# A one-hot gate product in a mixture-of-experts layer: two single-pass matmuls of a split gate, spread over 24 slots a tile

## What is computed

```
q = (xb @ w_q).reshape(blk, PEER_HEADS, 2, PEER_HALF)
s = jnp.einsum('thpd,phkd->thpk', q, sub_keys)
sv, si = lax.top_k(s, PEER_TOPK)
cand = sv[:, :, 0, :, None] + sv[:, :, 1, None, :]
cand_idx = si[:, :, 0, :, None] * N_KEYS + si[:, :, 1, None, :]
top_s, top_pos = lax.top_k(cand.reshape(...), PEER_TOPK)
idx = jnp.take_along_axis(cand_idx..., top_pos, axis=-1)
g = jax.nn.softmax(top_s, axis=-1)
act = gelu(einsum('thk d,td->thk', u_tab[idx], xb))
y = einsum('thk,thkd->td', g * act, v_tab[idx])
```

## Time and profile before

| | us |
|---|---|
| median of 3 runs | 4426.57 (4424.93 to 4427.05) |
| profiled execution | 4427.57 |
| its span | 4425.5 |
| PE busy | 4175.6 (94%) |
| PEld busy | 3762.6 (85%) |
| DVE busy | 2527.9 (57%) |
| ACT busy | 1179.3 (27%) |
| granted clock of PE, mean | 0.961 of 2.4 GHz |

### The profile page before, as it was taken

One profiled execution on the slowest core, in us unless ns is written; L12 is line 12 of the kernel. 1 busy time (PEld: TensorE's weight loads), 2 busy tenths in 40 slices (PEclk: granted clock), 3 DMA queues, 4 the chain that ended last, 5 costly groups with the idle time before them and its releaser, 6 DMA issues. The chain is left out here.

```text
span 4425.5 us, 74733 instructions
## 1 busy us (share of the span) xinstructions
PE 4175.6 (94%) x27369; PEld 3762.6 (85%) x27369; DVE 2527.9 (57%) x4678; ACT 1179.3 (27%) x1585; POOL 38.2 (1%) x43
## 2 busy tenths in 40 slices
PE   8778679999999999999998988999999999999998
PEld 8654479999999998888888567999999998888887
DVE  3742247777776435555544846787777525555553
ACT  2101132233333321121113443223333322111111
POOL 0000000000000010000000000000000001000000
PEclk9868789999999999999998989999999999999998
DMA  3026523335445565555532012334454466555551
GB/s 111 19 92 202 170 84 105 112 126 185 154 160 171 186 233 193 193 193 194 189 112 71 24 38 96 107 123 142 165 181 157 166 209 218 192 195 190 196 190 53
DMA packets 321925, 652.38 MB, mean 147 GB/s; under 512 B 26241, under 2 KB 157442, under 8 KB 321154
## 3 DMA queue, kind: packets, MB, share of 16 engines
q1 hardware_dynamic: 318978, 642.36, 43.1%
q0 software_dynamic: 2816, 8.40, 0.5%
HBM read 509.00 MB, written 141.53 MB: 147 GB/s over the span
## 5 line engine op out<-in xcount | busy, mean ns | idle before, releaser
L1781 DVE TENSOR_TENSOR experts_ul<-experts_u,experts_uh 128x1024 fp32r<-128x1024 f32 x512 | 627.1, 1225 | 1074.4 <-ACT experts_uh L1678 1068.0
L1578 PE MATMUL ps<-peer_x_then_r_xh,experts_ul 128*128 128x260 f32 x4096 | 1173.3, 286 | 0.0
L1579 PE MATMUL ps<-experts_over_x_xl,experts_uh 128*128 128x260 f32 x4096 | 1157.4, 283 | 0.0
L1580 PE MATMUL ps<-peer_x_then_r_xh,experts_uh 128*128 128x260 f32 x4096 | 1155.8, 282 | 0.0
L1678 ACT ACTIVATE experts_uh<-experts_u 128x1024 fp32r<-128x1024 f32 x512 | 540.8, 1057 | 1094.7 <-PE ps L1642 1085.2
L1641 PE MATMUL ps<-experts_over_a_al,experts_uh 128*128 128x512 f32 x2048 | 797.3, 389 | 0.0
L1642 PE MATMUL ps<-experts_over_a_ah,experts_uh 128*128 128x512 f32 x2048 | 797.3, 389 | 0.0
L1640 PE MATMUL ps<-experts_over_a_ah,experts_ul 128*128 128x512 f32 x2048 | 797.2, 389 | 0.0
L1579 PEld LDWEIGHTS ps<-experts_over_x_xl,experts_uh 128*128 128x128 f32 x4096 | 772.9, 189 | 0.0
L1578 PEld LDWEIGHTS ps<-peer_x_then_r_xh,experts_ul 128*128 128x128 f32 x4096 | 772.1, 189 | 0.0
L1580 PEld LDWEIGHTS ps<-peer_x_then_r_xh,experts_uh 128*128 128x128 f32 x4096 | 771.9, 188 | 0.0
(11 more groups left out here) (342 smaller groups left out, 4770.0 us busy)
## 6 DMA issues: line engine op xcount, KB each, us to landing
experts_u<-peer_u SPq DMA_DIRECT2D x256, 512.0 KB, 3.3
experts_u<-peer_v SPq DMA_DIRECT2D x256, 512.0 KB, 3.3
hidden<-experts_act SPq DMA_DIRECT2D x256, 260.0 KB, 2.2
gates<-experts_over_b_g SPq DMA_DIRECT2D x128, 512.0 KB, 3.0
experts_over_b_g<-gates SPq DMA_DIRECT2D x128, 512.0 KB, 5.0
experts_act<-hidden SPq DMA_DIRECT2D x256, 256.0 KB, 3.6
mla_ct<-cache SPq DMA_DIRECT2D x64, 320.0 KB, 3.8
pa_ct<-cache SPq DMA_DIRECT2D x64, 320.0 KB, 3.8
```

Source lines behind the costliest of these rows:

```text
L1578: pe.matmul(o, ul[:, b % 4, c], xh[:, c, t], start=(c == 0), stop=False)
L1579: pe.matmul(o, uh[:, b % 4, c], xl[:, c, t], start=False, stop=False)
L1580: mm = pe.matmul(o, uh[:, b % 4, c], xh[:, c, t], start=False, stop=(c == KC - 1))
L1781: v.tensor_tensor(ul[:, b % 4], u[:, b % 2], uh[:, b % 4].bitcast(F32), ALU.subtract).then_inc(split_done, 1)
```

## The change

`hidden` and its 128 slots stay. What changes is what stands beside them.

- **The gate product.** `cols[:, 2]` (the gate) is split once a tile into `gate_h` (fp32r) and the rest, by a copy and a subtraction on DVE. `one_hot` makes onej (now fp32r, two buffers), onei (now one buffer), and then **two** products, one_h = onei x gate_h and one_l = onei x rest, both fp32r. `gates` does two fp32r matmuls for each token (onej by one_h, onej by one_l), 16 a batch in place of 8 in fp32.
- **The slots.** Tiles have 24 slots in place of 20: batches in two of three (b % 3 of 1 and 2), none where b % 3 is 0. The first tile begins at slot 24 (before 32) and 8 slots are left at the end (before 16).
- **DVE's order.** For each b: `one_hot` for the batch of slot b + 1 where (b + 1) % 3 is not 0, then `low`, then the pieces of the selection, which stand two together in every third slot: `{2: (0, 1), 5: (2, 3), 8: (4, 5), 11: (6, 7), 14: (8, 9), 17: (10, 11), 20: (12,)}`. The samples' selection moves from slots 16 to 23 to a place beside the fourth tile.
- **The turn of the picks** comes at the first slot of a tile, just before `hidden`, and one slot ahead of the first batch.
- **The stores of the gates** are issued four at once, after every sixth slot.
- `rest`, `top` and `topi` move to another shared buffer.

```
-FIND, PLAIN, BATCHES = 16, 4, TT // BT
-PER_TILE = PLAIN + BATCHES
-ONES = FIND + 2 * BT
+FIND, BATCHES = 16, TT // BT
+PER_TILE = BATCHES * 3 // 2
+ONES = FIND + 8
...
                 with sp.Fori(0, NP) as t:
...
+                    first = ONES + PER_TILE * t
+                    for b in range(PER_TILE):
+                        plain(first + b, b)
+                        if b % 6 == 5:
+                            for c in range(4):
+                                store_gates(PT * t + b // 6, b // 6 % 2, c)
+                for n in range(TAIL, NK):
...
-                    if n == TAIL + PLAIN:
+                    if n == TAIL:
                         for b in range(2):
                             sp.wait_ge(g_stored[b], 16 * 4 * NQ // 2 + 64)
...
                 def gates(n, b):

-                    pe.wait_ge(one_ready, n + 1)
+                    pe.wait_ge(one_ready, n + 2)
                     for m in range(2):
                         pe.wait_ge(g_free, 2 * n + m + 1)
                         for e in range(4):
-                            mm = pe.matmul(k.ps[:, 4 + m, e * NK:(e + 1) * NK], onej[:, b % 2, 4 * m + e], onei[:, b % 2, 4 * m + e],
-                                           start=True, stop=True)
+                            o, at = k.ps[:, 4 + m, e * NK:(e + 1) * NK], 4 * m + e
+                            pe.matmul(o, onej[:, b % 2, at], one_h[:, b % 2, at], start=True, stop=False)
+                            mm = pe.matmul(o, onej[:, b % 2, at], one_l[:, b % 2, at], start=False, stop=True)
                         mm.then_inc(g_ready, 1)
...
                 with pe.Fori(0, NP) as t:
                     first = ONES + PER_TILE * t
...
+                    turn_picks(t)
+                    with pe.Fori(0, 2) as v:
+                        for b in range(PER_TILE // 2):
+                            if b % 3:
+                                a_ = b - 1 - b // 3
+                                gates(BATCHES * t + BATCHES // 2 * v + a_, a_)
+                            hidden(first + PER_TILE // 2 * v + b, b)
+                turn_picks(NP)
...
+                with act_e.Fori(0, NP) as t:
                     first = ONES + PER_TILE * t
+                    for b in range(PER_TILE):
+                        v = b // 6
+                        if b % 6 == 1:
+                            act_e.wait_ge(g_stored[v % 2], 64 * (2 * t + v // 2) + 64)
+                        if b % 3:
+                            a_ = b - 1 - b // 3
+                            copy_gates(BATCHES * t + a_, a_, v)
                         plain(first + b, b)
+                        if b == 10:
+                            exponentials(t + 1)
...
+                def one_hot(n, at, b):
+
+                    tok = slice(at, at + BT)
+                    v.wait_ge(g_ready, 2 * n + 2)
+                    v.tensor_tensor(onej[:, b % 2], bc(k.iota[:], 1, BT), bc(cols[:, 1, tok], 2, NK), ALU.is_equal)
+                    wait(v, one_ready, n + 1)
+                    v.tensor_tensor(onei[:], bc(k.iota[:], 1, BT), bc(cols[:, 0, tok], 2, NK), ALU.is_equal).then_inc(one_made, 1)
+                    wait(v, one_made, n + 1)
+                    v.tensor_tensor(one_h[:, b % 2], onei[:], bc(gate_h[:, tok].bitcast(F32), 2, NK), ALU.mult)
+                    v.tensor_tensor(one_l[:, b % 2], onei[:], bc(cols[:, 2, tok], 2, NK), ALU.mult).then_inc(one_ready, 1)
...
+                with v.Fori(0, NP) as t:
+                    chain = Chain(v, elink)
+                    first = ONES + PER_TILE * t
+                    v.wait_ge(turned, t + 1)
+                    v.tensor_copy(cols[:], turn).then_inc(cols_copied, 1)
+                    wait(v, cols_copied, t + 1)
+                    v.tensor_copy(gate_h[:], cols[:, 2]).then_inc(gate_ready, 1)
+                    wait(v, gate_ready, 2 * t + 1)
+                    v.tensor_tensor(cols[:, 2], cols[:, 2], gate_h[:].bitcast(F32), ALU.subtract).then_inc(gate_ready, 1)
+                    wait(v, gate_ready, 2 * t + 2)
+                    for b in range(PER_TILE):
+                        if (b + 1) % 3:
+                            a_ = b - b // 3
+                            one_hot(BATCHES * t + a_, BT * a_, a_)
+                        low(first + b + LOW, b + LOW)
+                        for piece in PIECES.get(b, ()):
+                            select(piece, t + 1, t + 1, chain, STEPS * (t + 1))
```

More of the change, by code:

```diff
@@ L1302, in peer_experts @@
         cols = s.sb("cols", [P, 3, TT])
+        gate_h = s.sb("gate_h", [P, TT], F32R)
         scols = s.sb("scols", [P, 3, TS])
@@ L1317, in peer_experts @@
         rows = over.row().sb("rows", [P, TS, D])
-        over = Overlay(nc, s, "over_a", 16384)
+        over = Overlay(nc, s, "over_a", 4 * 7 * BT * NK)
+        found = over.row()
+        rest = found.sb("rest", [TT, NT, NK])
+        top = found.sb("top", [TT, NT, TOPK])
+        topi = found.sb("topi", [TT, NT, TOPK], U32)
         first = over.row()
-        onej = first.sb("onej", [P, 2, BT, NK])
-        onei = first.sb("onei", [P, 2, BT, NK])
+        onej = first.sb("onej", [P, 2, BT, NK], F32R)
+        onei = first.sb("onei", [P, BT, NK])
+        one_h = first.sb("one_h", [P, 2, BT, NK], F32R)
+        one_l = first.sb("one_l", [P, 2, BT, NK], F32R)
         then = over.row()
@@ L1326, in peer_experts @@
         al = then.sb("al", [P, 2, TP], F32R)
-        over = Overlay(nc, s, "over_b", 33280)
+        over = Overlay(nc, s, "over_b", 32768)
         first = over.row()
@@ L1376, in peer_experts @@
         cols_copied = s.sem("cols_copied")
+        gate_ready = s.sem("gate_ready")
         one_made = s.sem("one_made")
@@ L1464, in plain @@
                     store(n, b)
[L1466 to L1470, removed]
-                with sp.Fori(0, NP) as t:
[L1472 to L1481, removed]
+                for n in range(FIND, ONES):
+                    plain(n, n)
+                with sp.Fori(0, NP) as t:
+                    first = ONES + PER_TILE * t
[5 more added lines that the diff above has]
+                for n in range(TAIL, NK):
                     if n + LOAD < NK:
@@ L1731, in exponentials @@
                     act_e.activation(expd[:], expd[:], ACT.Exp).then_inc(exped, 1)
[L1733 to L1739, removed]
                 def plain(n, b):
@@ L1743, in plain @@
                     gelu(n, b)
-                def tile(t, last=False):
-                    first = ONES + PER_TILE * t
-                    for b in range(PLAIN):
-                        plain(first + b, b)
[L1749 to L1760, removed]
+                for n in range(FIND, ONES):
+                    plain(n, n)
+                    if n == FIND + 4:
+                        exponentials(0)
+                with act_e.Fori(0, NP) as t:
+                    first = ONES + PER_TILE * t
+                    for b in range(PER_TILE):
[5 more added lines that the diff above has]
+                            copy_gates(BATCHES * t + a_, a_, v)
+                        plain(first + b, b)
+                        if b == 10:
+                            exponentials(t + 1)
                 for n in range(TAIL, NK):
@@ L1784, in _ @@
                 v.sem_inc(score_free, 1)
+                v.sem_inc(one_ready, 1)
                 slab_low(0, 0)
@@ L1908, in choose @@
                     assert chain.n == STEPS, chain.n
-                choose(0, NP, FIND, 0)
-                v.wait_ge(turned, 1)
+                choose(0, 0, FIND, 0)
+                def one_hot(n, at, b):
[7 more added lines that the diff above has]
+                    v.tensor_tensor(one_l[:, b % 2], onei[:], bc(cols[:, 2, tok], 2, NK), ALU.mult).then_inc(one_ready, 1)
+                PIECES = {2: (0, 1), 5: (2, 3), 8: (4, 5), 11: (6, 7), 14: (8, 9), 17: (10, 11), 20: (12,)}
+                with v.Fori(0, NP) as t:
[15 more added lines that the diff above has]
+                            select(piece, t + 1, t + 1, chain, STEPS * (t + 1))
+                    assert chain.n == STEPS
+                v.wait_ge(turned, NP + 1)
                 v.tensor_copy(scols[:], turn[:, :, 0:TS]).then_inc(cols_ready, 1)
@@ L1919, in _ @@
                 v.tensor_scalar(h_idx[:], at_of[:], float(TP), None, ALU.add).then_inc(idx_ready, 1)
[L1920 to L1955, removed]
                 def gate(m, b, par):
```

8 lines of the change are left out of this document (2 added, 6 removed).

## The result

| | before | after |
|---|---|---|
| median, us | 4425.75 (run beside it) | 4478.05 (4474.11 to 4480.86) |
| ratio | | 1.0115 [1.0102, 1.0128] |
| profiled execution / span, us | 4427.57 / 4425.5 | 4480.86 / 4479.0 |
| PE busy | 4175.6 (94%) | 4188.3 (94%) |
| DVE busy | 2527.9 | 2672.1 |

What follows compares the result with a forecast made beforehand. PE's own stream was taken as the bound. Product 0, waits 55.8 us and restarts 5.6, less 11.3 + 0.8, gave net +49 us: 4476 us, 1.1% slower; own range 4465 to 4492, with rivals 4422 to 4528.

Steps and rivals of the forecast that it cites:

- What bounds the kernel: In the tiles PE's own stream is the bound; PE waits only where one_hot comes late, 11.3 us before the change.
- Part 1: Gate product: 16 fp32r matmuls cost a batch 1.76 to 1.80 us, as now, bound by weight loads; 0 us taken.
- Part 2: Steady part of a tile: low, two pieces, then a longer one_hot make PE wait, 5.87 us a tile.
- Part 3: A tile's start: PE waits 1.10 us for the first one_hot behind the turn, bounds 0.7 to 1.6.
- Part 4: Samples' selection, ACT's work and four stores at once cost nothing while their cover lasts.
- rival D: The burst of stores delays u, 1 to 2 us in 32 places: 4508 to 4540; chance 8%.
- The sum: Whole kernel: waits 55.8 us and restarts 5.6, less 11.3 + 0.8 that go; net +49 us, 4476 median.
- Restarts: After each PE wait in the tiles, 0.1 us more; 7 x 8 x 0.1 = 5.6 us.
- rival C: The clock falls at the larger waits beside half-streaming gates: 32 falls, +51 us, 4527; chance 6%.
- Rival A: Waits inside the tiles don't appear, low coming earlier or pieces being covered; only the start remains: 4424; chance 11%.
- B: Gate product: fp32r matmuls stream, not bound by the load; a batch falls to 0.94 us: 4366; chance 9%.
- The case on which 66% stood: The forecast itself: DVE's order and longer one_hot make PE wait, product unchanged; 4476 us, own range 4465 to 4492.

Runs made afterwards that it cites:

- the kernel with the pieces ahead: The kernel after, with the selection pieces moved before low on DVE in every third slot; 4422.38 us, ratio 0.999.
- the split product in the old slots: The kernel before, with the split, four operations and 16 fp32r matmuls, keeping its 20 slots, DVE order and spread stores; 4468.06 us, ratio 1.0092.

## Why the prediction was right, and where it was off

**What bounds the kernel**, and what an idle PE costs: held. No other engine than DVE, and no DMA, ended a wait of PE in the tiles.

**Part 1, 0 us for the product**: held, 0.11 us a load in fp32r too, with all 128 columns and with 32. The two rules of the Trainium skill's "TensorE: Matmul & The Clock Gate" part here. Its section "LDWEIGHTS (loading the stationary operand)" gives P / 1.2 ns for a load of P columns, from which 107 ns for 128 columns is an estimate, and the trace agrees (110 to 112). The 81 ns of "Back-to-back issue gap" are not reached by any batch of fp32 or fp32r here, not even with few columns: no two loads of a batch start less than 107 ns apart.

**Part 2, DVE's order**: this step carried the forecast and held. The waits by slot, from the start of `hidden` to the start of the next batch, less the 5.75 us without a wait, mean of 8 tiles:

| slot of the tile | forecast | measured |
|---|---|---|
| 1 (start) | 1.10 | 0.98 |
| 4 | 1.67 | 1.44 |
| 7 | 0.41 | 0.17 |
| 10 | 0.73 | 0.57 |
| 13 | 0.2 | 0.86 |
| 16 | 1.43 | 1.19 |
| 19 | 1.43 | 1.27 |
| sum | 6.97 | 6.48 |

Five of the six in the steady part are 0.16 to 0.24 too high. The part that they share is `low`, which begins 3.52 behind the batch (905.81 - 902.29) where 3.66 was taken; besides, some pairs are up to 0.08 shorter than they were taken (the first 5.11, 912.06 - 906.95, for 5.18). The one_hot's 4.97 came out as 4.96. Slot 13 is the term that was mis-sized: the forecast took ACT's way to `low` for the same in every triple, and ACT has the exponential in one of them, with a table load of 1.28 us ahead of it (968.03) and another behind. The first is on the path: the copies of the batch come behind it (969.54), `high` behind them (970.50), and `low` 0.86 us later than elsewhere. The second comes when `high` is done, and delays nothing: the gelu behind it waits another 2.10 us for PE. The Trainium skill's "ScalarE activation tables: per-element evaluation and per-set limits", section "What a function is on this engine", gives 1283 ns for such a load, and the trace agrees. The statement that ACT "has 207 of 577 us" and so costs nothing was an average over slots; in this one slot ACT was on the path.

**Part 3, the start**: 0.98 for 1.10. From the turn (887.68) to the one_hot 2.00 for 2.20.

**Part 4**: held, but for ACT's exponential. The gates' stores land in 4.4 us where they took 3.0, and neither PE nor ACT waits for a DMA in the tiles: rival D's burst is in the kernel with the pieces ahead too, at 4422.

**The sum.** Waits 6.48 x 8 = 51.8 for 55.8. Restarts: from the batch's start to `hidden` 1.83 us behind a wait and 1.74 without, 56 x 0.09 = 5.0 for 5.6. Less the 12.1 of the waits of before. That is 44.7. From the start of `hidden(16)` to that of `hidden(127)` the two layers take 1576.0 us where they took 1520.8, 55.2 more. The rest is **rival C, in part**: seven falls of the clock. One of them, behind the wait of 1.02 at slot 16 (windows; columns as in the earlier trace rows, PEclk the third from the right):

```profile
1003.00:1005.00 2.00, 1.52 (x14) 1.52 (x14) 2.00 (x3) 0.47 (x2) 0.00 (x0) 1.00 0.00 0
1005.00:1007.00 2.00, 2.00 (x14) 2.00 (x14) 1.90 (x3) 1.71 (x3) 0.00 (x0) 0.68 0.65 123
1007.00:1009.00 2.00, 2.00 (x12) 2.00 (x11) 2.00 (x2) 0.06 (x1) 0.00 (x0) 0.50 0.71 268
1009.00:1011.00 2.00, 2.00 (x18) 2.00 (x18) 1.36 (x2) 0.00 (x0) 0.00 (x0) 0.97 0.01 4
```

The clock goes to the lower level (1.2 GHz) for some 3 us, and `hidden` takes 7.33 us from 1005.32 to 1012.65 where it takes 5.8. All seven stand behind the waits at slots 4, 16 and 19. They cost 7 x 1.53 = 10.7, and 44.7 + 10.7 = 55.4 for 55.2. The spans differ by 53.5, since the rest of the program, in which the change only moves buffers, took 1.7 us less in this execution. The forecast gave C only as a whole case, 32 falls or none; a few falls belonged in the sum. It priced a fall at 1.6 us as 16 gate matmuls at half speed. The size is right, but by luck: the gate matmuls are over by 1005.32, and it is the `hidden` behind them that runs slowly. The waits and restarts were put 5 us too high and the clock 11 too low, so the total of +49 for +52 came out closer than its terms; that closeness is luck, the 56 waits are not.

Rival A (the waits don't appear) was refuted by the 56 waits, B by loads that stand 0.11 us apart with 128 columns and with 32, D by the burst that cost nothing. The case on which 66% stood is shown, not only argued: taking away the order alone ends the waits at slots 4 to 19, and taking away the fourth operation leaves 0.2 to 0.5 us of them at slots 4, 16 and 19.

## What to carry to other kernels

Where one engine feeds the one that bounds the kernel, an average of free time says little: write down when each operand is ready and when it is wanted, slot by slot, and put work whose inputs are there ahead of an operation that a third engine releases late. Here one moved call was worth 56 us. The gate products here, of 128 columns and fewer, are paid by their weight loads, so a split into two cheap passes that loads twice brought nothing. And look for the slot in which a helper engine does something rare, such as a table load.

## What the hardware showed that was not expected

- **The clock can fall behind a gap of 1 us.** In the kernel after 7 of the 24 larger waits (1.0 to 1.3 us and 16 fp32r matmuls of 128 columns behind them) were followed by a fall of some 3 us, 1.5 us lost each. With 32 columns in the second product 2 of 8 waits of 0.7 to 0.8 us were; with 128 columns none of 8 such waits. In the split product in the old slots every tile's start was (2.7 to 3.2 us of gap). With the same 56 waits and the product in full fp32 there was none. What decides between waits that are followed by a fall and waits that aren't stays open.
- **A long loop on PE costs at its jump back**: 4.9 us each by the medians (2.5 to 4.8 in the profiled execution) with 24 slots of 48 matmuls and more written out, no such row with 12.
- **fp32r loads of 128 columns stand 0.11 us apart, with 128 columns streamed and with 32**, also when the operand loaded is the one that was just used: the loads at 902.18 and 902.29 have the same onej.
